# Expert rows are added to a DRAM table by an accumulating indirect DMA instead of by a matmul

## The chip, the cores and the metric

One core of one Trainium2 chip runs the whole program in one launch. The metric is device time in microseconds (us), lower is better: the median of three runs. A profiled execution gives the trace that is read here; it has a time of its own, which stands beside its span below.

## The reference

Two layers. Each mixes 256 tokens of width 1024 by four groups of attention, adds a projection and normalises, and then runs a mixture of experts. Only that last part is touched by the change:

```
scores = sigmoid(x @ w_router); sel = top 8 of (scores + router_bias) of 64 experts
gates  = scores[sel] / sum(scores[sel]) * 2.5          # 0 for experts not chosen
routed = sum over e of ((silu(h[:, :256]) * h[:, 256:]) * gates[e]) @ w_down[e],  h = x @ w_gu[e]
x      = layer_norm(ALPHA * x + routed + shared)       # shared: one more expert, without gate
```

An expert's weights are 3 MB: w_gu is 1024 x 512 and w_down 256 x 1024, in f32.

## The kernel before

**Order of the experts.** All 64 experts are ranked by how many tokens chose them. NIT = 16 steps take four experts each, in four classes. Expert A of a step (the busiest 16) is computed densely, for all 256 tokens. Expert B (the next 16) is computed for at most 128 gathered tokens, one per partition; these are "the 128 places". Experts C1 and C2 have at most 64 tokens each and share the 128 partitions. A step therefore reads 12 pieces of 1 MB: B0, B1 (the two halves of B's w_gu), A0, C10, C20, A1, C11, C21, then the four w_down, BD, AD, C1D, C2D.

**Weights.** SyncE loads the pieces in this order into a ring of six slots (`raw`, line 540). Piece j goes into slot j % 6 and is issued when TensorE has used the piece six before it (`unit_used`). So B0 and B1 of the next step are issued once C11 and C21 of this step, which one loop of products uses (line 1044), are done with. Matmuls run in fp32r, a faster format with fewer bits; for A and B each piece is split in two: ScalarE casts it to fp32r (`high`, line 1365), VectorE subtracts that from the original (`low`, line 1717). C's products are plain f32 and read the ring directly.

**A step on TensorE** (from line 1009): B's gate and up product (line 1018), A's with A0 (lines 910 to 912), the transposes of B's activations (line 1034), C with C10 and C20 (line 1044), A with A1, C with C11 and C21, B's down product into banks 0 and 1 (line 1059), the transposes of C's activations (line 1065), A's down product into the four banks 4 to 7 that hold the sums of all tokens (line 933), `scatter(place_b, t)` (line 947), C's down product into banks 2 and 3 (line 1085), the transposes of the next B tokens `xg_b` into banks 0 and 1 (line 940), `scatter(place_c, t)`, the transposes of the next C tokens `xg_c`.

**How rows get back to their tokens.** The 128 rows of B's output stand in slot order. `place_b` is a 0/1 matrix of 128 places by 256 tokens. `scatter` multiplies it with the output and adds to the banks of sums: 2 tiles x 2 halves x 2 parts = 8 matmuls of 512 columns. The two parts are `o_hi`, the ScalarE cast of the output (lines 1404 and 1406 for B, 1413 and 1415 for C), and `o_lo`, the rest, by VectorE (`out_lo`, line 1745). B and C use the same `o_hi` and `o_lo`, one after the other.

**The order on the other engines** is written out by hand, and each engine runs it in order. VectorE near the end of a step: `low(it, AD)`, C's activation `a_c` (line 1776), `out_lo` for B, `low(it+1, B0)`, `low(it+1, B1)`, `out_lo` for C, the low part of the gathered B tokens (line 1725), `low(it+1, A0)`, then the next step with `places` (lines 1736, 1737). ScalarE: the two casts of B's output, the copy `at_c`, `high(it+1, B0)`, `high(it+1, B1)`, the two casts of C's output, the cast of the gathered tokens (line 1371). GpSimd, in the experts' part, only gathers the next step's tokens from the DRAM table `x_rows` (lines 657, 659), after `tokens` on VectorE has made the indices (lines 1692 to 1696). Its DMAs run on queue q0 (software), SyncE's on q1, and both on the same 16 DMA engines.

Of the kernel before, what the change touches and what calls it, by code (L numbers as in the profile page):

```python
# [19 lines left out]
F32 = mybir.dt.float32  # L20
F32R = mybir.dt.float32r
I32 = mybir.dt.int32
U32 = mybir.dt.uint32
# [4 lines left out]
P = 128  # L28
# [8 lines left out]
def build(nc, x, w_in, b_forget, mla_q_norm, mla_kv_norm, w_mla_uq, w_mla_ukv, t5_rel_bias,  # L37
# [71 lines left out]
    with ctx:  # L109
# [92 lines left out]
        token_b = sb("token_b", [P, 1], U32, where=mo)  # L202
        token_c = sb("token_c", [P, 1], U32, where=mo)
        ranked = sb("ranked", [NE, 2, SEQ], where=mo)
        by_expert = sb("by_expert", [NE, 2, SEQ], where=mo)
# [4 lines left out]
        rank = sb("rank", [NE, 1], where=mo)  # L210
        perm = sb("perm", [NE, NE], where=mo)
        sh_down = sb("sh_down", [P, UNIT_F], where=list(mo))
        sh_down_r = sb("sh_down_r", [P, UNIT_F], F32R, where=mo)
        assert mo[0] <= nc.sbuf_usable_end, (mo[0], nc.sbuf_usable_end)
        assert shared_end <= nc.sbuf_usable_end, (shared_end, nc.sbuf_usable_end)
# [58 lines left out]
        ps = ctx.enter_context(nc.psum_tensor("ps", [P, 8, 512], F32))  # L274
        x_rows = nc.dram_tensor("x_by_token", (SEQ, D), F32, kind="Internal").ap()
        t5_dram = nc.dram_tensor("t5_by_distance", (NH, HANKEL), F32, kind="Internal").ap()
# [122 lines left out]
        b_half_ps = layer_sem("b_half_ps", NIT)  # L399
        b_out_hi_sb = layer_sem("b_out_hi_sb", 2 * NIT)  # L400
        b_out_sb = layer_sem("b_out_sb", 2 * NIT)
# [3 lines left out]
        b_added = layer_sem("b_added", NIT)  # L405
        tile0_done = layer_sem("tile0_done", 1)
# [193 lines left out]
        def _(pool):  # L600
# [5 lines left out]
            pool.memset(ones[:], 1.0).then_inc(consts_built, 1)  # L606
            pool.iota(token_row[:], [[1, SEQ]], base=0, channel_multiplier=0, allow_small_or_imprecise_dtypes=True)
            pool.iota(slot_col[:, 0:1], [[0, 1]], base=1, channel_multiplier=1, allow_small_or_imprecise_dtypes=True)
# [8 lines left out]
            for c, (base, step) in enumerate(((0, 1), (NIT, 1), (2 * NIT, 2), (2 * NIT + 1, 2))):  # L617
# [10 lines left out]
            pool.affine_select(out=head_rows[:], in_=head_rows[:], compare_op=ALU.not_equal, fill=1.0, base=0,  # L628
                               pattern=[[-1, NH], [0, P]], channel_multiplier=1).then_inc(consts_built, 1)
            with pool.Fori(0, DEPTH) as layer:  # L630
                def split_lo(k, before):

                    for half in range(2):
                        full, hi, lo = half_of(k, half)
                        pool.wait_ge(w_hi_ready, done(layer, w_hi_ready, before + half + 1))
                        pool.tensor_tensor(lo, full, hi, ALU.subtract).then_inc(w_lo_ready, 1)  # L636
# [16 lines left out]
                pool.sem_inc(pool_turn, 1)  # L653
                with pool.Fori(0, NIT) as it:
                    pool.wait_ge(token_ready, done(layer, token_ready, it + 1))
                    pool.sem_inc(pool_turn, 1)
                    pool.indirect_dma_start(xg_b[:], None, x_rows, bass.IndirectOffsetOnAxis(ap=token_b[:, 0:1], axis=0))\  # L657
                        .then_inc(xg_b_loaded, 16)
                    pool.indirect_dma_start(xg_c[:], None, x_rows, bass.IndirectOffsetOnAxis(ap=token_c[:, 0:1], axis=0))\
                        .then_inc(xg_c_loaded, 16)  # L660

        @prog.tensor
        def _(pe):
# [45 lines left out]
            with pe.Fori(0, DEPTH) as layer:  # L709
# [299 lines left out]
                def step(it, final):  # L1009
# [102 lines left out]
        def _(act):  # L1112
# [6 lines left out]
            with act.Fori(0, DEPTH) as layer:  # L1119
# [268 lines left out]
                def step(it, final):  # L1388
# [14 lines left out]
                    act.wait_ge(b_half_ps, done(layer, b_half_ps, it + 1))  # L1403
                    nc.scalar.copy(o_hi[:, 0:512], ps[:, 0, :]).then_inc(b_out_hi_sb, 1)
                    act.wait_ge(unit_used, used(layer, it, BD))
                    nc.scalar.copy(o_hi[:, 512:D], ps[:, 1, :]).then_inc(b_out_hi_sb, 1)
                    act.wait_ge(c_t_ps, done(layer, c_t_ps, it + 1))
# [22 lines left out]
        def _(dve):  # L1430
            nc.vector.memset(zeros[:].bitcast(F32), 0.0)
            dve.wait_ge(consts_built, 6)

            def layer_norm(layer, t, bank, signal, roots):

                xt = x_tok[:, t, :]
                nc.vector.scalar_tensor_tensor(xt, xt, ALPHA, ps[:, bank:bank + 2, :].rearrange("p a n -> p (a n)"),
                                               ALU.mult, ALU.add)
# [16 lines left out]
            with dve.Fori(0, DEPTH) as layer:  # L1455
# [181 lines left out]
                for t in range(NT):  # L1637
                    dve.wait_ge(outproj_ps, done(layer, outproj_ps, 1 + NOUT * t))
                    layer_norm(layer, t, OUT_BANK[t], x_mid, 2 + t)
                for b in range(4):  # L1640
# [48 lines left out]
                def tokens():  # L1689

                    for i, row in enumerate((row_b, row_c)):
                        nc.vector.scalar_tensor_tensor(found[:, i, :], row[:, 1, :], slot_col[:, i:i + 1], token_row[:],
                                                       ALU.is_equal, ALU.mult, accum_out=token[:, i:i + 1])
                    dve.drain()
                    nc.vector.tensor_copy(token_b[:], token[:, 0:1])
                    nc.vector.tensor_copy(token_c[:], token[:, 1:2]).then_inc(token_ready, 1)  # L1696

# [50 lines left out]
                def step(it, final):  # L1748

                    places(place_b, row_b, gate_b, 0).then_inc(place_b_ready, 1)  # L1750
                    dve.wait_ge(xc_ps, done(layer, xc_ps, it + 1))
                    places(place_c, row_c, gate_c, 1).then_inc(place_c_ready, 1)
# [9 lines left out]
                    if not final:  # L1762
# [28 lines left out]
                for t in range(NT):  # L1791
                    if t == 0:
                        dve.wait_ge(tile0_done, done(layer, tile0_done, 1))
                    else:
                        dve.wait_ge(moe_done, done(layer, moe_done, 1))
                    layer_norm(layer, t, 4 + 2 * t, x_next, 4 + t)

# [51 lines left out]
```

## Time and profile before

| | us |
|---|---|
| median of 3 runs (1814.83 to 1820.38) | 1816.24 |
| the profiled execution | 1813.22 |
| its span | 1811.4 |
| TensorE busy (share of the span) | 1712.4 (95%) |
| VectorE busy | 986.2 (54%) |
| ScalarE busy | 768.0 (42%) |
| GpSimd busy | 227.4 (13%) |
| DMA, mean rate over the span | 281 GB/s |
| software queue q0, share of the 16 DMA engines | 6.0% |

The busy time of an engine is a union of its instructions; a busy TensorE is not one at its peak. The two stretches with the experts run from about 210 to 905 us and from about 1120 to 1800 us. Idle time of an engine matters only where something that sets the end waits for it.

### The profile page before, as it was taken

Reading aid. Unit: us, or ns where it says so; the run is one execution under the profiler, and the core shown is the slowest. Engines: PE = TensorE matmul, PEld = TensorE weight load, DVE = VectorE, ACT = ScalarE, POOL = GpSimd, SP = SyncE. Lnnn points to the kernel's source line nnn. Section 1 sums busy time; section 2 is a strip of 40 time slices with the busy share of each in tenths; the row PEclk is TensorE's granted clock in tenths of the full one; section 3 lists DMA queues with packets and bytes.
Section 4 is the critical chain, followed back from the end, with each engine's and each line's share of the span. In section 5 each row is a group of like instructions: output and inputs, shape, how many; then the busy total and the mean of one; then the engine's idle time right before and its main releaser. Section 6 shows DMA issues by size and latency. Waiting matters only on the chain.

```text
span 1811.4 us, 29520 instructions
## 1 busy us (share of the span) xinstructions
PE 1712.4 (95%) x10302; PEld 1302.3 (72%) x10302; DVE 986.2 (54%) x1441; ACT 768.0 (42%) x1020; POOL 227.4 (13%) x160
## 2 busy tenths in 40 slices
PE   7798999999999999999979988999999999999996
PEld 6687766777777777767677876777776777777774
DVE  2746455555555555555457555555555555555554
ACT  4464333443444434444346634443444444334331
POOL 6380000000000000000144700000000000000000
PEclk8898999999999999999989989999999999999998
DMA  8232699889899989888853228888888898888983
GB/s 286 85 130 65 222 337 328 331 332 333 334 338 332 335 333 335 333 330 320 290 173 114 97 70 325 330 334 336 336 332 335 317 327 336 330 322 334 330 322 116
DMA packets 136091, 509.26 MB, mean 281 GB/s; under 512 B 11588, under 2 KB 50920, under 8 KB 102760
## 3 DMA queue, kind: packets, MB, share of 16 engines
q1 hardware_dynamic: 122288, 467.77, 70.0%
q0 software_dynamic: 9792, 35.66, 6.0%
q10 hardware_dynamic: 3960, 5.17, 0.9%
q8 instruction: 30, 0.49, 0.1%
q14 instruction: 21, 0.17, 0.0%
HBM read 505.14 MB, written 3.41 MB: 281 GB/s over the span
## 4 chain that ended last, share of the span: by engine, by line
PE 81%; DVE 7%; DMA 4%; ACT 3%; DVEq 2%; issue 2%; ACTq 0%; SPq 0%; PEldq 0%
PE ps L1044 11%; PE ps L933 10%; PE ps L1018 10%; PE ps L910 7%; PE ps L947 7%; PE ps L911 7%; PE ps L912 7%; PE ps L1085 6%; PE ps L694 5%; PE ps L1059 5%; DMA raw<-in_w_exp_down_dram 2%; PE ps L940 2%; PE ps L826 1%; DVE o_lo L1745 1%; DMA raw<-in_w_exp_gu_dram 1%
## 5 line engine op out<-in xcount | busy, mean ns | idle before, releaser
L1717 DVE TENSOR_TENSOR raw_r<-raw,w_hi 128x2048 fp32r<-128x2048 f32 x192 | 439.9, 2292 | 397.6 <-ACT w_hi L1365 397.6
L1365 ACT CAST w_hi<-raw 128x2048 fp32r<-128x2048 f32 x192 | 365.7, 1906 | 286.7 <-DMA raw<-in_w_exp_down_dram 175.5
L910 PE MATMUL ps<-x_hi,w_hi 128*128 128x256 f32 x1088 | 311.4, 286 | 1.8 <-DVE x_lo L1643 1.8
L911 PE MATMUL ps<-x_lo,w_hi 128*128 128x256 f32 x1088 | 306.9, 282 | 0.0
L912 PE MATMUL ps<-x_hi,raw_r 128*128 128x256 f32 x1088 | 306.2, 281 | 0.0
L1044 PE MATMUL ps<-raw,xc 128*64 128x512 f32 x1024 | 233.8, 598 | 0.0
L910 PEld LDWEIGHTS ps<-x_hi,w_hi 128*128 128x128 f32 x1088 | 206.6, 190 | 31.4 <-issue 30.1
L911 PEld LDWEIGHTS ps<-x_lo,w_hi 128*128 128x128 f32 x1088 | 207.9, 191 | 1.5
L912 PEld LDWEIGHTS ps<-x_hi,raw_r 128*128 128x128 f32 x1088 | 206.7, 190 | 0.0
L657 POOL DMA_INDIRECT xg_b<-x_by_token,token_b x32 | 30.1, 940 | 1248.2 <-DVE token_c L1696 1248.2
L1044 PEld LDWEIGHTS ps<-raw,xc 128*64 128x64 f32 x1024 | 67.8, 136 | 119.4 <-issue 115.0
L1745 DVE TENSOR_TENSOR o_lo<-ps,o_hi 128x512 fp32r<-128x512 f32 x128 | 87.8, 688 | 58.2 <-ACT o_hi L1415 24.3
L933 PE MATMUL ps<-w_hi,a_hi 128*128 128x512 f32 x272 | 112.2, 413 | 6.3 <-DVE a_lo L1703 6.3
L1085 PE MATMUL ps<-raw,at_c 128*64 128x512 f32 x512 | 116.9, 598 | 0.0
L933 PE MATMUL ps<-w_hi,a_lo 128*128 128x512 f32 x272 | 107.9, 397 | 0.0
L1018 PE MATMUL ps<-w_hi,xb_hi 128*128 128x512 f32 x256 | 102.5, 401 | 1.3 <-DVE xb_lo L1725 1.3
L933 PE MATMUL ps<-raw_r,a_hi 128*128 128x512 f32 x256 | 101.0, 395 | 0.0
L1018 PE MATMUL ps<-raw_r,xb_hi 128*128 128x512 f32 x256 | 100.5, 392 | 0.0
L1018 PE MATMUL ps<-w_hi,xb_lo 128*128 128x512 f32 x256 | 99.8, 390 | 0.0
L1085 PEld LDWEIGHTS ps<-raw,at_c 128*64 128x64 f32 x512 | 33.9, 136 | 66.6 <-issue 66.6
L636 POOL TENSOR_TENSOR raw_r<-raw,w_hi_odd 128x1024 fp32r<-128x1024 f32 (+1 forms) x28 | 68.6, 2471 | 63.5 <-ACT w_hi_odd L1126 63.5
L694 PE MATMUL ps<-x_hi,raw_r 128*128 128x256 f32 (+2 forms) x256 | 74.9, 293 | 0.0
(314 smaller groups left out, 2962.3 us busy)
## 6 DMA issues: line engine op xcount, KB each, us to landing
raw<-in_w_exp_gu_dram SPq DMA_DIRECT2D x256, 1024.0 KB, 6.4
raw<-in_w_exp_down_dram SPq DMA_DIRECT2D x128, 1024.0 KB, 7.5
raw<-in_w_in_dram SPq DMA_DIRECT2D x22, 1024.0 KB, 5.8
raw<-in_w_out_dram SPq DMA_DIRECT2D x8, 1024.0 KB, 5.1
row_b<-gates_by_rank SPq DMA_DIRECT2D x30, 256.0 KB, 5.7
row_c<-gates_by_rank SPq DMA_DIRECT2D x60, 128.0 KB, 5.3
raw<-in_w_sh_gu_dram SPq DMA_DIRECT2D x4, 1024.0 KB, 5.4
row_a<-gates_by_rank SPq DMA_DIRECT2D x32, 128.0 KB, 8.1
```

The costliest lines, as they stand in the source:

```text
L694: last = nc.tensor.matmul(o, a, b, start=(c == 0 and i == 0), stop=(c == KC - 1 and i == 2))
L910: nc.tensor.matmul(o, h, x_hi[:, c, :], start=(first and i == 0), stop=False, skip_group_check=True)
L911: nc.tensor.matmul(o, h, x_lo[:, c, :], start=False, stop=False, skip_group_check=True)
L912: last = nc.tensor.matmul(o, l, x_hi[:, c, :], start=False, stop=(final and i == 3), skip_group_check=True)
L933: last = nc.tensor.matmul(ps[:, 4 + 2 * t + half, :], lhs, rhs, start=False, stop=False, skip_group_check=True)
L947: last = nc.tensor.matmul(ps[:, 4 + 2 * t + half, :], place[:, t * P:(t + 1) * P], part[:, half * 512:(half + 1) * 512], start=False, stop ...
L1018: last = nc.tensor.matmul(ps[:, 2, :], a[:, c, :], b[:, i, :], start=(c == 0 and k == 0), stop=(c == KC - 1 and k == 2))
L1044: last = nc.tensor.matmul(ps[HALF * h:HALF * (h + 1), 3, :], xc[:, c, HALF * h:HALF * (h + 1)], piece_slot(j % RING, u)[:, i, :], start=(c ...
L1085: last = nc.tensor.matmul(ps[HALF * h:HALF * (h + 1), 2 + half, :], at_c[:, c, HALF * h:HALF * (h + 1)], piece_slot(j % RING, 2)[:, c, hal ...
L1365: nc.scalar.copy(w_hi[CAST[j] % 3][:], raw[:, j % RING, 0:UNIT_F]).then_inc(hi_done, 1)
L1717: nc.vector.tensor_tensor(raw_r[:, s, 0:UNIT_F], raw[:, s, 0:UNIT_F], w_hi[CAST[j] % 3][:], ALU.subtract)\
L1745: nc.vector.tensor_tensor(o_lo[:, part], ps[:, bank + half, :], o_hi[:, part], ALU.subtract)\
```

## The change

B's output no longer goes through `place_b` in 15 of the 16 steps of a layer. ScalarE copies it as f32 into a tile of its own, `o_b`. VectorE computes for each place a row number `token_out`: the token's, or for an empty place a spare row of its own behind the table. GpSimd adds the 128 rows of `o_b` to a DRAM table `added_rows` with one indirect DMA with `compute_op=add`. The table is cleared from `zeros` at the start of each layer; some spare rows are set once. After the 15th scatter GpSimd loads the table (1 MB) into `added`, and in the last step VectorE forms ALPHA * x + added before the layer norm, which then has scale 1. The last step keeps the product. For the spare rows, token numbers are counted from -256 and 256 is added where a row number is wanted; an empty place gathers a zero row behind `x_rows`.

```diff
+            pool.sem_inc(o_b_free, START[o_b_free])
+            pool.wait_ge(zeros_ready, 1)
+            pool.dma_start(x_rows[SEQ].rearrange("(p n) -> p n", n=P), zeros[0:D // P, :].bitcast(F32)).then_inc(spare_row_stored, 16)
+            pool.dma_start(added_rows[SEQ + 1:SEQ + 1 + P, :].rearrange("p (c n) -> p c n", n=P),
+                           zeros[:].bitcast(F32).unsqueeze(1).to_broadcast([P, KC, P])).then_inc(spare_row_stored, 16)
+            pool.wait_ge(spare_row_stored, 32)
             with pool.Fori(0, DEPTH) as layer:
+                for t in range(NT):
+                    pool.dma_start(added_rows[t * P:(t + 1) * P, :].rearrange("p (c n) -> p c n", n=P),
+                                   zeros[:].bitcast(F32).unsqueeze(1).to_broadcast([P, KC, P])).then_inc(sums_cleared, 16)
...
+                gather(0)
+                with pool.Fori(0, NIT - 1) as it:
+                    gather(it + 1)
+                    pool.wait_ge(o_b_ready, done(layer, o_b_ready, it + 1))
+                    pool.sem_inc(pool_turn, 1)
+                    pool.indirect_dma_start(added_rows, bass.IndirectOffsetOnAxis(ap=token_out[:, 0:1], axis=0), o_b[:], None,
+                                            compute_op=ALU.add).then_inc(o_b_added, 16)
+                    pool.wait_ge(o_b_added, done(layer, o_b_added, it * 16 + 16))
+                    pool.sem_inc(o_b_free, 1)
+                for t in range(NT):
+                    pool.dma_start(added[:, t, :], added_rows[t * P:(t + 1) * P, :]).then_inc(sums_loaded, 16)
+                pool.wait_ge(sums_loaded, done(layer, sums_loaded, 16 * NT))
...
 TensorE:
-                    pe.wait_ge(place_b_ready, done(layer, place_b_ready, it + 1))
-                    pe.wait_ge(b_out_sb, done(layer, b_out_sb, it * 2 + 2))
-                    for t in range(NT):
-                        last = scatter(place_b, t)
-                    last.then_inc(b_added, 1)
+                    if final:
+                        pe.wait_ge(place_b_ready, done(layer, place_b_ready, it + 1))
+                        pe.wait_ge(b_out_sb, done(layer, b_out_sb, 2))
+                        for t in range(NT):
+                            scatter(place_b, t)
...
                     if not final:
+                        pe.wait_ge(o_b_ready, done(layer, o_b_ready, it + 1))
                         pe.wait_ge(xg_b_loaded, done(layer, xg_b_loaded, it * 16 + 32))
 ScalarE:
+                    else:
+                        act.wait_ge(o_b_free, done(layer, o_b_free, it))
+                        nc.scalar.copy(o_b[:, 0:512], ps[:, 0, :])
+                        act.wait_ge(unit_used, used(layer, it, BD))
+                        nc.scalar.copy(o_b[:, 512:D], ps[:, 1, :]).then_inc(o_b_ready, 1)
 VectorE:
+                    if not final:
+                        dve.wait_ge(o_b_free, done(layer, o_b_free, it))
+                        nc.vector.tensor_scalar(spare[:], token[:, 0:1], 0.0, slot_col[:, 0:1], ALU.is_equal, ALU.mult)
+                        dve.drain()
+                        nc.vector.scalar_tensor_tensor(token_out[:], spare[:], float(SEQ), token[:, 0:1], ALU.add, ALU.add)
...
+                    if final:
+                        dve.wait_ge(sums_loaded, done(layer, sums_loaded, 16 * NT))
+                        for t in range(NT):
+                            nc.vector.scalar_tensor_tensor(x_tok[:, t, :], x_tok[:, t, :], ALPHA, added[:, t, :], ALU.mult, ALU.add)
...
-                    out_lo(b_out_hi_sb, b_out_sb, it, 0)
+                    if final:
+                        out_lo(b_out_hi_sb, b_out_sb, 0, 0)
```

## Rows read from the trace of the kernel before

**Rows 1.** Busy time by stretch: PE, PEld, DVE, ACT, POOL (x instructions), clock, DMA share, GB/s

```profile
210.00:860.00 650.00, 641.55 (x3611) 465.86 (x3610) 357.66 (x465) 265.85 (x285) 28.10 (x30) 1.00 0.90 332
1120.00:1755.00 635.00, 627.20 (x3522) 454.04 (x3519) 351.80 (x456) 262.81 (x282) 28.08 (x30) 1.00 0.90 333
```

**Rows 2.** The chain that ended last, 500 to 580: start, us, what

```profile
514.87 2.09 PE ps L947 x8
...
550.98 1.86 PE ps L947 x8
552.83 3.63 PE ps L1085 x16
556.49 0.59 ACT o_hi L1415
557.11 0.70 DVE o_lo L1745
557.81 0.14 issue
557.95 2.10 PE ps L947 x8
```

**Rows 3.** What line 1745 waited for, whole run: us in total, times

```profile
  ACT o_hi L1415: 24.3, 30
  ACT o_hi L1413: 18.8, 5
```

**Rows 4.** Timeline of VectorE in one step: start, us, line, what [idle before <-releaser]

```profile
553.67 2.29 DVE L1717 TENSOR_TENSOR raw_r<-raw,w_hi 128x2048 fp32r<-128x2048 f32 x1 [0.18 <-ACT w_hi L1365]
555.88 0.68 DVE L1745 TENSOR_TENSOR o_lo<-ps,o_hi 128x512 fp32r<-128x512 f32 x1
557.11 0.69 DVE L1745 TENSOR_TENSOR o_lo<-ps,o_hi 128x512 fp32r<-128x512 f32 x1 [0.54 <-ACT o_hi L1415]
...
562.66 0.35 DVE L1736 TENSOR_SCALAR place_b<-row_b,slot_col 128x256 fp32r<-128x256 f32 x1
```

**Rows 5.** Timeline of ScalarE, same step

```profile
545.20 0.58 ACT L1406 CAST o_hi<-ps 128x512 fp32r<-128x512 f32 x1 [0.77 <-PE ps L1059]
...
551.74 1.90 ACT L1365 CAST w_hi<-raw 128x2048 fp32r<-128x2048 f32 x1 [0.57 <-DMA raw<-in_w_exp_gu_dram]
554.75 0.58 ACT L1413 CAST o_hi<-ps 128x512 fp32r<-128x512 f32 x1 [1.11 <-PE ps L1085]
```

**Rows 6.** Timeline of SyncE and of TensorE, same step

```profile
542.43 3.29 SPq L540 DMA_DIRECT2D raw<-in_w_exp_gu_dram  x3
...
538.56 3.65 PE L1044 MATMUL ps<-raw,xc 128*64 128x512 f32 x16
```

**Rows 7.** DMA queue of 546 to 552: packets, MB, share of 16 engines

```profile
q1 hardware_dynamic: 339, 2.52, 100.2%
```

**Rows 8.** DMA queues and gathers of 531 to 545 (issue to landing)

```profile
q1 hardware_dynamic: 1065, 4.16, 74.6%
q0 software_dynamic: 288, 1.05, 23.3%
...
xg_b<-x_by_token,token_b POOLq DMA_INDIRECT x1, 4.8
xg_c<-x_by_token,token_c POOLq DMA_INDIRECT x1, 8.6
```

**Rows 9.** DMA queue of 172.5 to 174.5, a store of 128 rows to DRAM

```profile
q0 software_dynamic: 144, 0.52, 64.7%
```

**Rows 10.** Timeline: the index of a gather on VectorE, the gather on GpSimd

```profile
531.05 0.14 DVE L1696 CAST token_c<-token 128x1 uint32<-128x1 f32 x1
...
531.98 0.94 POOL L657 DMA_INDIRECT xg_b<-x_by_token,token_b  x1 [40.92 <-DVE token_c L1696]
```

**Rows 11.** Last step of a layer: timelines of VectorE and TensorE, then the chain

```profile
889.66 0.47 DVE L1776 SCALAR_TENSOR_TENSOR a_c<-silu_c,gate_c,ps 128x256 f32<-128x256 f32 x1
...
890.98 0.38 PE L1065 MATMUL ps<-ident,a_c 128*128 128x128 f32 x2
...
905.20 1.22 DVE x_tok L1437
```

**Rows 12.** Start: DMA queues of 10 to 38, timelines of VectorE and GpSimd

```profile
q1 hardware_dynamic: 7296, 7.37, 81.4%
q10 hardware_dynamic: 1848, 2.43, 26.3%
...
38.04 4.19 DVE L1467 TENSOR_TENSOR band_bias<-hankel,block 128x256 f32<-128x256 f32 x4 [24.65 <-DMA ln_b<-in_ln_b_dram]
...
13.23 1.04 POOL L643 CAST w_hi_even<-raw 128x1024 fp32r<-128x1024 f32 x1 [8.05 <-DMA raw<-in_w_in_dram]
```

More of the change, by code:

```diff
@@ L203, in build @@
         token_c = sb("token_c", [P, 1], U32, where=mo)
+        token_out = sb("token_out", [P, 1], U32, where=mo)
+        spare = sb("spare", [P, 1], where=mo)
         ranked = sb("ranked", [NE, 2, SEQ], where=mo)
@@ L211, in build @@
         perm = sb("perm", [NE, NE], where=mo)
+        o_b = sb("o_b", [P, D], where=list(mo))
         sh_down = sb("sh_down", [P, UNIT_F], where=list(mo))
         sh_down_r = sb("sh_down_r", [P, UNIT_F], F32R, where=mo)
+        added = sb("added", [P, NT, D], where=mo)
         assert mo[0] <= nc.sbuf_usable_end, (mo[0], nc.sbuf_usable_end)
@@ L274, in build @@
         ps = ctx.enter_context(nc.psum_tensor("ps", [P, 8, 512], F32))
[L275 removed]
+        x_rows = nc.dram_tensor("x_by_token", (SEQ + 1, D), F32, kind="Internal").ap()
+        added_rows = nc.dram_tensor("sums_by_token", (SEQ + 1 + P, D), F32, kind="Internal").ap()
         t5_dram = nc.dram_tensor("t5_by_distance", (NH, HANKEL), F32, kind="Internal").ap()
@@ L399, in build @@
         b_half_ps = layer_sem("b_half_ps", NIT)
-        b_out_hi_sb = layer_sem("b_out_hi_sb", 2 * NIT)
-        b_out_sb = layer_sem("b_out_sb", 2 * NIT)
+        b_out_hi_sb = layer_sem("b_out_hi_sb", 2)
+        b_out_sb = layer_sem("b_out_sb", 2)
         c_half_ps = layer_sem("c_half_ps", NIT)
@@ L404, in build @@
         c_out_sb = layer_sem("c_out_sb", 2 * NIT)
-        b_added = layer_sem("b_added", NIT)
+        zeros_ready = sem("zeros_ready")
+        spare_row_stored = sem("spare_row_stored")
+        sums_cleared = layer_sem("sums_cleared", 16 * NT)
+        o_b_ready = layer_sem("o_b_ready", NIT - 1)
+        o_b_added = layer_sem("o_b_added", 16 * (NIT - 1))
+        o_b_free = layer_sem("o_b_free", NIT - 1, 1)
+        sums_loaded = layer_sem("sums_loaded", 16 * NT)
         tile0_done = layer_sem("tile0_done", 1)
@@ L653, in _, with gather @@
                 pool.sem_inc(pool_turn, 1)
-                with pool.Fori(0, NIT) as it:
+                pool.wait_ge(sums_cleared, done(layer, sums_cleared, 16 * NT))
+                pool.sem_inc(pool_turn, 1)
+                def gather(it):
                     pool.wait_ge(token_ready, done(layer, token_ready, it + 1))
@@ L1403, in step @@
                     act.wait_ge(b_half_ps, done(layer, b_half_ps, it + 1))
-                    nc.scalar.copy(o_hi[:, 0:512], ps[:, 0, :]).then_inc(b_out_hi_sb, 1)
-                    act.wait_ge(unit_used, used(layer, it, BD))
-                    nc.scalar.copy(o_hi[:, 512:D], ps[:, 1, :]).then_inc(b_out_hi_sb, 1)
+                    if final:
+                        nc.scalar.copy(o_hi[:, 0:512], ps[:, 0, :]).then_inc(b_out_hi_sb, 1)
+                        act.wait_ge(unit_used, used(layer, it, BD))
+                        nc.scalar.copy(o_hi[:, 512:D], ps[:, 1, :]).then_inc(b_out_hi_sb, 1)
+                    else:
+                        act.wait_ge(o_b_free, done(layer, o_b_free, it))
+                        nc.scalar.copy(o_b[:, 0:512], ps[:, 0, :])
+                        act.wait_ge(unit_used, used(layer, it, BD))
+                        nc.scalar.copy(o_b[:, 512:D], ps[:, 1, :]).then_inc(o_b_ready, 1)
                     act.wait_ge(c_t_ps, done(layer, c_t_ps, it + 1))
@@ L1430, in _, with layer_norm @@
         def _(dve):
-            nc.vector.memset(zeros[:].bitcast(F32), 0.0)
+            nc.vector.memset(zeros[:].bitcast(F32), 0.0).then_inc(zeros_ready, 1)
             dve.wait_ge(consts_built, 6)
-            def layer_norm(layer, t, bank, signal, roots):
+            def layer_norm(layer, t, bank, signal, roots, scale):
                 xt = x_tok[:, t, :]
-                nc.vector.scalar_tensor_tensor(xt, xt, ALPHA, ps[:, bank:bank + 2, :].rearrange("p a n -> p (a n)"),
+                nc.vector.scalar_tensor_tensor(xt, xt, scale, ps[:, bank:bank + 2, :].rearrange("p a n -> p (a n)"),
                                                ALU.mult, ALU.add)
@@ L1638, in _ @@
                     dve.wait_ge(outproj_ps, done(layer, outproj_ps, 1 + NOUT * t))
-                    layer_norm(layer, t, OUT_BANK[t], x_mid, 2 + t)
+                    layer_norm(layer, t, OUT_BANK[t], x_mid, 2 + t, ALPHA)
                 for b in range(4):
@@ L1694, in tokens @@
                     dve.drain()
-                    nc.vector.tensor_copy(token_b[:], token[:, 0:1])
-                    nc.vector.tensor_copy(token_c[:], token[:, 1:2]).then_inc(token_ready, 1)
+                    nc.vector.tensor_scalar(token_b[:], token[:, 0:1], float(SEQ), None, ALU.add)
+                    nc.vector.tensor_scalar(token_c[:], token[:, 1:2], float(SEQ), None, ALU.add).then_inc(token_ready, 1)
                 def dense_gated(n):
@@ L1795, in _ @@
                         dve.wait_ge(moe_done, done(layer, moe_done, 1))
-                    layer_norm(layer, t, 4 + 2 * t, x_next, 4 + t)
+                    layer_norm(layer, t, 4 + 2 * t, x_next, 4 + t, 1.0)
 _INS = ["x", "w_in", "b_forget", "mla_q_norm", "mla_kv_norm", "w_mla_uq", "w_mla_ukv", "t5_rel_bias",
```

5 lines of the change are left out of this document (4 added, 1 removed).

## The prediction

> **What bounds the kernel now.** I read the busy time by stretch first. In the two long stretches of experts TensorE is busy 641.55 of 650 us and 627.20 of 635 us at a granted clock of 1.00, and the 16 DMA engines 0.90 of the time [rows 1]. So TensorE looks like the bound, with the DMA close behind. An average says nothing on where in a step either of them has room; for that I read the chain of waits and then the timelines of one step.
>
> The chain shows one period: the C scatter starts at 514.87 and the next one at 557.95, so a step takes 43.08 us [rows 2]. The reader is to see the hand-over at its end. TensorE finishes C's down product (line 1085), ScalarE casts the second half (0.59), VectorE takes the low part (0.70), 0.14 passes, and TensorE scatters C. The eight matmuls of the B scatter, at 550.98, take 1.86 us of the chain [rows 2]. They are what the change removes.
>
> Next I ask who would be late if C's down product came 1.86 us sooner. VectorE reaches the first half of C's `out_lo` at 555.88, straight from the split of B1 of the next step (553.67, 2.29 us), with no idle time before it [rows 4]. Only between the two halves does it wait for ScalarE, here 0.54 us. Over the whole run it waited there 24.3 us in 30 steps, 0.81 us each, and before the first half only 5 times in 32 [rows 3]. VectorE is in order, so the 0.81 us is all it can come earlier, as long as B1's split is where it is. That split is tied to a transfer: ScalarE casts B1 at 551.74, after waiting for the DMA [rows 5], and B0 and B1 are issued from 542.43, when TensorE ends the C products that begin at 538.56 and last 3.65 us [rows 6]. I call that end T0 (542.2). In times after T0: B1 cast 9.5, its split over 13.8, `o_lo` 15.2 at the earliest, C scatter 15.75. The issue at T0 does not move when the B scatter, which comes after it, goes.
>
> So the loop that would bind next is T0, transfer of B0 and B1, cast, split, `out_lo`, C scatter, and then TensorE without a gap to the next T0.
>
> **The change part by part.**
>
> *The B scatter goes* from 30 steps (15 per layer): 30 x 1.86 = 55.8 us off TensorE [rows 2]. By the loop above only 0.81 x 30 = 24.3 us of it can become time [rows 3]; for the rest TensorE would stand waiting for `o_lo`. VectorE also loses two `out_lo` of 0.69 us per step, but it waits for the DMA after them anyway, so that is worth nothing.
>
> *The scatter DMA comes*, 0.5 MB in 128 rows of 4 KB, on q0. When? ScalarE ends its second copy at 545.78 [rows 5], T0 + 3.6. From the end of `token_c` (531.19) to the gather that waits for it (531.98) pass 0.8 us [rows 10], so it is issued at T0 + 4.4, and the first of its packets I put near T0 + 6. At that moment DMA is full: from 546 to 552 q1 alone has 100.2% of the 16 engines [rows 7]. Still due are the end of B0 and all of B1, about 3 us of transfer. Whatever engine time the scatter takes before B1 has landed, B1 lands later by that, and by the loop so does everything in the step.
>
> That the two queues share the engines packet by packet, instead of q0 waiting its turn, the gathers show: in 531 to 545 q0 took 23.3% and q1 74.6%, together 98%, and the first gather landed 4.8 us after its issue with weight loads in front of it [rows 8]. The Trainium skill ("DMA: Bandwidth & Descriptors", section "Queues, rings and completion order") says that each engine takes turns between the queues it has work for, a whole packet at a time. Its example packet of 9 to 17 descriptors would let all eight rows of an engine pass in one turn; the delay of B1 would be the same.
>
> *What the scatter costs in engine time* no row shows, as the kernel has no accumulating DMA. The nearest rows: storing 128 rows to DRAM took 64.7% of 2 us = 1.29 us of all 16 engines [rows 9]; gathering 128 rows took 23.3% of 14 us, halved for two gathers = 1.63 us [rows 8]. A plain scatter would therefore cost 1.3 to 1.6. The add must read both the row in SBUF and the row in DRAM before it writes; I take two transfers, 2 x 1.29 = 2.58 us. The low end is 0, if it starts so late that B1 is already in; a high end of 4 x 1.29 = 5.2 leaves room for an adder that is slower than the copy. The same page (section "SDMA does more than copy") lists ADD as an elementwise reduce of two streams; that is the same factor of two, and no row here shows it.
>
> *Net of a step:* 2.58 - 0.81 = +1.77 us, and 30 x 1.77 = +53 us. TensorE's removed 1.86 us and the new delay of 2.58 turn into a wait of about 3.6 us before every C scatter.
>
> *New waits on `o_b_free`.* The DMA is done 4.8 to 8.6 us after issue by the gathers [rows 8], say up to 12: T0 + 9 to 16. VectorE asks for it when `place_b` is over, 562.66 + 0.8, T0 + 21 [rows 4], with all of the next B and C activations queued behind it; ScalarE and GpSimd ask later. Free, unless the add takes over 16 us. The two added one-column VectorE operations (0.15 each by the casts of [rows 10], and a drain) fall where VectorE waits 3 us for `silu_b`: nothing. `o_b_ready` before the transposes of `xg_b` is 7 us old when TensorE asks. GpSimd gathers before it scatters, so the gathers don't move.
>
> *Last step.* VectorE puts two 1024-wide operations before `a_c`. The like operation of the layer norm takes 1.22 [rows 11]. `a_c` moves from 889.66 to 892.1 and ends at 892.6, and TensorE wanted it at 890.98: 1.7 us, twice = +3.4 us. The load of the table is issued some 30 us earlier and hidden.
>
> *Start.* GpSimd now stores 0.5 MB, waits, and clears 1 MB before it can copy the first weights at 13.23 [rows 12]. From 10 to 38 the engines are full (81.4% + 26.3%), and VectorE stands from the start until 38.04 for the landing of the last parameters [rows 12]. Small packets cost 26.3% of 28 us for 2.43 MB, 3.0 us a MB; the 0.5 MB fall mostly before 10, the 1.05 MB not: 3.2 us on that landing. Bounds 0 and 10 (GpSimd issues 1024 short pieces per DMA; should that be slow, its first split is late too). In the second layer the clears fall beside the last step of the first, off the chain: 0, at most 3.
>
> *Sum:* 1813.2 + 53 + 3.4 + 3.2 = 1873 for the profiled execution. The median shown is 3.0 above that execution, so **1876 us**.
>
> **The rivals.**
>
> *A. TensorE is the bound and the DMA costs nothing on the path.* For it: 641.55 of 650 busy [rows 1]. All 1.86 us would be saved: 1816 - 55.8 + 6.6 = 1767. Against it: it needs B1's split 1 us earlier than any transfer in the trace brings it, and VectorE came to `o_lo` without a wait in 27 of 32 cases [rows 3]. Chance 0.05.
>
> *B. Faster, but by the VectorE loop only.* The scatter's packets start after B1 has landed, or fill holes. The point from which it decides is a delay of 0.81 us: below it the change is faster. At delay 0: 1816 - 24.3 + 6.6 = 1799. For it: the start near T0 + 6 is inferred, and GpSimd may need longer for an address list on the writing side; 3 us later would do. Chance 0.11.
>
> *C. Break-even.* Delay 0.6 to 0.8 us (half of a plain scatter falls in front of B1): 1810 to 1822. Chance 0.07.
>
> *D. The forecast:* delay 1.0 to 3.3 us, 1829 to 1898. Chance 0.60.
>
> *E. The adder is slow:* delay over 3.3 us, up to 5.2 and more. At 5.2, 30 x 4.4 = 132, so 1955. An even slower one runs into the `o_b_free` waits. Nothing in the trace speaks for or against. Chance 0.17.
>
> **How the numbers follow.** The most likely is D with 1876. The range of 8 in 10 leaves out A, most of B and the slow half of E: 1808 to 1945. A change within 0.3% (5.4 us) can't be told from none. Faster: A and B, 0.16. Same: C, 0.07. Slower: D and E, 0.77.
>
> **What would show it.** In the trace after: no B scatter in the loop, a period near 44.9 us instead of 43.08, ScalarE's cast of B1 near T0 + 12 instead of 9.5, and TensorE idle about 3.6 us before the first C scatter with VectorE's `o_lo` as releaser. If the cast of B1 stays at T0 + 9.5, the delay is wrong and B holds. If TensorE goes from C's down product to the C scatter with the old wait and a period of 41.2, A holds and my loop is wrong. A share of q0 in 546 to 552 gives the price of the add. `a_c` of the last step should end about 2.4 us later relative to its neighbours, and the first `band_bias` should start near 41.

## The result and the profile after

| | before | after |
|---|---|---|
| median | 1815.53 us (8 runs) | 1802.15 us (8 runs) |
| ratio | | 0.9926, 95% interval 0.9898 to 0.9953 |
| span of the profiled execution | 1811.4 | 1799.5 |

The change is 0.7% faster, some 13 us. I forecast 60 us slower, so the prediction was wrong in sign; the time that came is that of its rival B (1799). All times after T0 below are counted, as in the prediction, from the end of the products of line 1044 (1083 in the new kernel).

First the page of the kernel after, its busy times, DMA queues and two groups.

```profile
PE 1664.7 (93%) x10062; PEld 1260.4 (70%) x10062; DVE 952.0 (53%) x1445; ACT 765.8 (43%) x1020; POOL 283.5 (16%) x200
...
q0 software_dynamic: 15440, 56.11, 11.2%
...
L692 POOL DMA_INDIRECT sums_by_token<-o_b,token_out x30 | 48.2, 1607 | 379.4 <-ACT o_b L1452 379.4
...
L986 PE MATMUL ps<-o_hi,place_c 128*128 128x512 f32 x128 | 53.5, 418 | 41.4 <-DVE o_lo L1791 41.4
```

TensorE has 47.7 us less to do (1712.4 before), and the span is only 11.9 us shorter. 25 us of the rest stand in the last row: the first matmul of the C scatter now waits 41.4 us for `o_lo`, which it did for 16.2 before.

Busy time by stretch, to hold against [rows 1]: the DMA share has risen from 0.90 to 0.95 and 0.96.

```profile
210.00:860.00 650.00, 625.01 (x3519) 450.95 (x3519) 347.65 (x470) 269.71 (x290) 54.07 (x47) 0.99 0.95 347
1120.00:1745.00 625.00, 601.40 (x3401) 432.35 (x3400) 335.78 (x454) 262.07 (x282) 52.27 (x46) 1.00 0.96 351
```

The chain of one step, against [rows 2]:

```profile
502.00 8.55 DMA raw<-in_w_exp_gu_dram
510.58 1.91 ACT w_hi L1405
512.51 0.12 DVE raw_r L1763
...
514.72 1.29 DVE o_lo L1791 x2
516.01 0.14 issue
516.15 2.09 PE ps L986 x8
```

The split stands in the chain only as pieces (a wait and "issue"); the timeline of VectorE shows it whole, and both halves of `o_lo` right behind it:

```profile
512.51 2.29 DVE L1763 TENSOR_TENSOR raw_r<-raw,w_hi 128x2048 fp32r<-128x2048 f32 x1 [0.18 <-ACT w_hi L1405]
514.72 1.28 DVE L1791 TENSOR_TENSOR o_lo<-ps,o_hi 128x512 fp32r<-128x512 f32 x2
```

Before, the chain reached the C scatter from TensorE's C down product over ScalarE and one `o_lo`. Now it comes from the transfer of B1, its cast, its split and both halves of `o_lo` without a gap: the loop that the prediction named. T0 is 501.1 here; B1's cast starts at T0 + 9.4, the C scatter at T0 + 15.0. Over 28 steps the period is 42.48 us on average (43.14 before), B1 lands at T0 + 9.48 (9.35), and the C scatter starts 5.60 us after that landing (6.46).

What line 1791 (1745 before) waited for shows it too, against [rows 3]. VectorE no longer waits for ScalarE between the halves in 30 steps, but in 4.

```profile
  ACT o_hi L1459: 18.8, 3
  ACT o_hi L1461: 3.4, 4
```

Where is the scatter DMA? GpSimd issues it at 505.52, T0 + 4.4 as forecast. The DMA queues of 501 to 510, then of 510 to 516:

```profile
q1 hardware_dynamic: 688, 3.83, 102.5%
```

```profile
q1 hardware_dynamic: 316, 1.40, 59.5%
q0 software_dynamic: 144, 0.52, 43.9%
```

Up to 510 there is no packet of q0, 4.5 us after the issue. From 510 on it takes 43.9% of 6 us = 2.63 us of all engines. B1 lands at 510.56. So the add costs what was forecast (2.58), but misses B1. Read packet by packet over all 30 adds of the trace, the first packet starts 4.83 us after the issue (median; T0 + 9.3), and of 2.65 us of engine time a mean of 0.10 falls before B1 has landed.

Where the 11.9 us of the span are, from the starts of the C scatters (us): the 28 repeated steps -18.4; up to the first C scatter of the first layer +5.1 (256.43 to 261.54), although this stretch too has lost a B scatter; the last steps of the layers +3.5 and +1.5; between the layers -3.6 (243.87 to 240.26); the sum is -11.9. Of the -3.6, about 1.9 is the B scatter of the second layer's first step, which is not among the 28; the rest is no more than single traces of kernels with the same work there differ by (243.87, 241.12 and 244.79 in the kernel before and its two other orders).

### The profile page after: what moved, and what is told of

It is laid out like the page before. It is cut to its first block, busy times and chain, and to the rows that moved or that the text cites. A ratio compares the mean times of both kernels' runs of the same rounds, so it can differ in the third digit from the quotient of the medians.

```text
span 1799.5 us, 29297 instructions
## 1 busy us (share of the span) xinstructions
PE 1664.7 (93%) x10062; PEld 1260.4 (70%) x10062; DVE 952.0 (53%) x1445; ACT 765.8 (43%) x1020; POOL 283.5 (16%) x200
## 4 chain that ended last, share of the span: by engine, by line
PE 64%; DMA 15%; DVE 7%; issue 5%; ACT 5%; DVEq 2%; SPq 1%; ACTq 0%; PEldq 0%
DMA raw<-in_w_exp_gu_dram 11%; PE ps L1083 11%; PE ps L1057 10%; PE ps L949 7%; PE ps L950 7%; PE ps L951 7%; PE ps L733 6%; PE ps L986 4%; PE ps L972 4%; ACT w_hi L1405 3%; DMA raw<-in_w_exp_down_dram 3%; DVE o_lo L1791 2%; PE ps L1124 2%; PE ps L979 2%; PE ps L865 1%
## 5 line engine op out<-in xcount | busy, mean ns | idle before, releaser
L692 POOL DMA_INDIRECT sums_by_token<-o_b,token_out x30 | 48.2, 1607 | 379.4 <-ACT o_b L1452 379.4
L986 PE MATMUL ps<-o_hi,place_c 128*128 128x512 f32 x128 | 53.5, 418 | 41.4 <-DVE o_lo L1791 41.4
```

The costliest lines, as they stand in the source:

```text
L986: last = nc.tensor.matmul(ps[:, 4 + 2 * t + half, :], place[:, t * P:(t + 1) * P], part[:, half * 512:(half + 1) * 512], start=False, stop ...
```

## The experiments

Periods and landings below are means over 28 steps of the one profiled execution, times are medians of timed runs; ratios are to the kernel before on the same chip. A period also holds steps that start with TensorE's granted clock below full: one of the 28 in the change, two in run 2, seven in run 4, three in run 6. Without them the periods are 42.43 in the change, 42.19 in run 2, 42.46 in run 4 and 42.50 in run 6, each uncertain by about 0.1.

**1. The three kinds of DMA by themselves.** A small kernel, GpSimd issuing one DMA after the other, VectorE and TensorE idle.

```
pool.indirect_dma_start(table, IndirectOffsetOnAxis(index), rows_out[:], None)                      # plain store
pool.indirect_dma_start(rows_in[:], None, table, IndirectOffsetOnAxis(index))                       # gather
pool.indirect_dma_start(table, IndirectOffsetOnAxis(index), rows_out[:], None, compute_op=ALU.add)  # add
```

(The index argument is shortened; after each DMA GpSimd waits for its landing.)

> Computes nothing of the reference: it copies x out and times three DMAs of 128 rows of 4 KB on GpSimd, four of each, each waited for: a plain indirect store, a gather, and an add, first on an idle chip, then beside SyncE loading 1 MB pieces one at a time, then with three always issued. Theory G (the add's late start comes from GpSimd's own work for it): on the idle chip the add already needs about 3 us more from issue to landing than the plain store (4.5 to 5 against about 8.5), and the deeper load queue adds only the time that the engines share, about 2.5 us. Theory Q (its packets wait behind the loads that are already queued on the engines): idle, the add needs only its extra transfer, 1.3 us more than the plain store (about 6), and with three loads issued every kind, gathers too, starts 3 us or more later than with one.

Issue to landing, median of four (of two for the idle plain store, whose first two ran beside the copies of x):

| | idle | one 1 MB load issued at a time | three always issued |
|---|---|---|---|
| plain store | 3.3 us | 5.3 | 8.5 |
| gather | 3.9 | 5.5 | 8.5 |
| add | 6.0 | 5.9 | 10.2 |

Answer for the add on the idle chip, then with three loads (min/median/max), and the DMA share of the four idle adds (34.8 to 59.6):

```profile
DMA to landing us min/median/max: 5.9/6.0/6.1
...
DMA to landing us min/median/max: 9.5/10.2/10.4
```

```profile
q0 software_dynamic: 576, 2.10, 54.0%
```

Theory Q holds against G: idle, the add needs nothing near the 8.5 of theory G, and behind three loads every kind is late, the plain store by 5.2 us. The add itself costs more than Q gave it: 2.7 us over the plain store when idle, of which 0.6 is GpSimd's own instruction (1.56 against 0.95 us).

A landing is late both because the packets start late and because they share the engines. The packets themselves tell the two apart. From issue to the first packet, in us:

| | idle | one load | three loads |
|---|---|---|---|
| plain store | 1.5 | 2.6 | 4.2 |
| gather | 1.6 | 2.3 | 4.2 |
| add | 2.1 | 2.1 | 4.8 |

So the start is 1.6 to 2.6 us later with three loads than with one, less than the 3 that Q asked for; only the landings are 3.0 to 4.3 later. Counted from the end of GpSimd's instruction, the first packet comes after 0.6 to 0.7 us when idle and after 3.2 us behind three loads, for all three kinds. The add of the change (4.83 us from issue, an instruction of 1.61) has the same 3.2.

**2. Without the scatter DMA.**

```diff
-                    pool.indirect_dma_start(added_rows, ..., o_b[:], None, compute_op=ALU.add).then_inc(o_b_added, 16)
-                    pool.wait_ge(o_b_added, done(layer, o_b_added, it * 16 + 16))
```

> Leaves out the scatter DMA (B's rows are never added); all else as in the changed kernel, and o_b_free is signalled at once. Theory L (the period is set by T0, transfer of B1, cast, split, o_lo, C scatter, and the scatter's packets come too late to delay B1): the period stays within 0.2 us of the changed kernel's 42.4, the C scatter starts 5.6 us after B1's landing as there, and the time is within 6 us of 1802. Rival S (the scatter's DMA takes part of the gain in every step by sharing the engines): without it the period falls toward 41.2 and the time by 15 us or more, to below 1787.

1792.55 us, ratio 0.9872 (0.9847 to 0.9898), against 0.9926 for the change. The period is 42.29 (42.48 with the DMA), B1 lands at 9.24 (9.48), the C scatter again 5.59 after it. So the loop stands without any scatter traffic, and S's 1787 and 41.2 are not reached. But 10 us is more than L allowed, and the trace shows about 7 of them: 28 x 0.2 = 5 us go with B1's landing (0.24 earlier), and the last step of the first layer takes 44.5 instead of 46.6. The traced execution also took 1804.24 us, the longest of the five, with 250.59 us between the layers, where the change has 240.26; its span can't be compared.

**3. The scatter DMA 4 us earlier.**

```diff
-                    pool.wait_ge(o_b_ready, done(layer, o_b_ready, it + 1))
+                    pool.wait_ge(a_ready, done(layer, a_ready, it + 2))
...
-                        nc.scalar.copy(o_b[:, 0:512], ps[:, 0, :])
+                        nc.scalar.copy(o_hi[:, 0:512], ps[:, 0, :])
```

(The second half likewise; `o_b` is set to zero once, so the DMA adds zeros and B's rows are left out.)

> The same adding DMA is issued about 4 us earlier in each step, at T0, from a tile of zeros (B's rows are not added; ScalarE copies them to o_hi as before). Its packets should start near T0 + 5 in place of T0 + 9.2. Theory L: now they stand in front of B1, which lands 2.6 us later (12.0 instead of 9.4 after T0), and the period grows by the same, 42.4 to about 45.0; 30 steps give +78 us, 1802 to about 1880. Rival S (shared bandwidth as such sets the time, not the place): the same bytes at another place change nothing, 1802 within 6 us.

1920.42 us, ratio 1.0599 (1.0555 to 1.0643). B1 lands at 11.63, 2.15 later than in the change, and the C scatter comes 5.59 after it. The first packet of the add starts at T0 + 6.8 (median), and 2.46 of its 2.64 us of engine time fall before B1's landing. Place decides, not bytes: S is out. But the period grew by 4.16 us, to 46.64, not by 2.15 as L had it (1880). The timeline of TensorE in one step, then the busy time by stretch:

```profile
491.41 1.16 PE L985 MATMUL ps<-ident,xg_b 128*128 128x128 f32 x8
496.46 0.77 PE L992 MATMUL ps<-o_hi,place_c 128*128 128x512 f32 x1 [3.90 <-DVE o_lo L1797]
497.03 0.63 PE L992 MATMUL ps<-o_lo,place_c 128*128 128x512 f32 x1
```

```profile
486.00:496.00 10.00, 6.57 (x33) 3.21 (x31) 5.47 (x4) 7.01 (x7) 0.00 (x0) 0.99 1.03 365
496.00:502.00 6.00, 5.54 (x17) 4.69 (x18) 4.70 (x10) 0.58 (x2) 0.00 (x0) 0.50 0.66 279
```

After 3.9 us of idling TensorE goes on at a granted clock of 0.50, the 1.2 GHz level: a matmul of the C scatter takes 0.63 us instead of 0.39, the group of eight 3.75 instead of 2.1. In 29 of the 30 steps other than a layer's last the clock falls like this, after waits of 2.3 to 4.6 us; its mean over the 6 us from the C scatter on is then 0.50 to 0.76. The other 2.0 us of a period are there: from the C scatter to the next T0 a step takes 29.4 us on average, 27.4 in the change. With its delay right my forecast would still have been short: about 46.6 a step and not 44.9.

**4. A plain store in place of the add.**

```diff
-                    pool.indirect_dma_start(added_rows, ..., o_b[:], None, compute_op=ALU.add)
+                    pool.indirect_dma_start(added_rows, ..., o_b[:], None)
```

> The scatter DMA without the add (a plain store of the rows, so the sums are not formed). Theory G: the packets start 1.6 us after issue like those of a gather, T0 + 6, cost 8 x 0.16 = 1.3 us of the engines before B1 has landed, and the step is 1.3 us longer than now although the DMA is the cheaper one: about +35 us, 1837. Theory Q: they start as late as those of the add, T0 + 9, and the time stays within 6 us of 1802.

1811.14 us, ratio 0.998 (0.9956 to 1.0004); B1 lands at 9.53, as with the add. So it is not the add that is late: the plain store too starts behind the queued loads (8.6 us to landing, a gather 5). Its first packet comes at T0 + 8.6, not at the T0 + 6 of theory G, and 0.66 before that of the add, which is what GpSimd's instruction is shorter by (0.99 against 1.61). The time is 9 us above Q's 1802, of which at most 6 were allowed, and far from G's 1837. The period is 42.90 with a mean clock of 0.98 and 0.99 in the long stretches, 1.00 in the change; one step with its C scatter at 389.05 ran its first 5 us at 0.66. Seven of the 28 steps begin like that here, after 1.9 to 2.8 us of waiting, and one in the change. These seven take 44.2 us on average and the other 21 take 42.46, as in the change (42.43), so the whole excess over the change is the clock. Why it fell more often here is open.

**5. VectorE's order.** `out_lo` of C ahead of the split of B1, in the changed kernel and in the kernel before.

```diff
                     if not final:
                         low(it + 1, B0)
-                        low(it + 1, B1)
                     out_lo(c_out_hi_sb, c_out_sb, it, 2)
                     if not final:
                         gathered_lo(it + 1, 0)
+                        low(it + 1, B1)
                         low(it + 1, A0)
```

> The changed kernel with VectorE's order alone altered at the end of a step: low(B0), out_lo of C, the low part of the gathered tokens, and only then low(B1), low(A0). Theory L (in the changed kernel the C scatter stands 5.6 us after B1's landing because out_lo is queued behind the split of B1): the C scatter leaves B1's landing, comes about 14.0 us after T0 in place of 15.1, the period falls from 42.4 to about 41.3 and the time by about 30 us, to 1770. Rival M (the C scatter waits for the shared DMA engines or for GpSimd's scatter itself): nothing changes, 1802 within 5 us.

> The kernel before with the same new order on VectorE. Theory L (there TensorE sets the C scatter, VectorE has 0.8 us to spare): the period stays 43.1 and the time within 5 us of 1814. Rival V (the order is a gain by itself, whatever the change): the period falls by 1 us and the time by 30.

Both missed. On the change: 1806.65 us, ratio 0.994 (0.9918 to 0.9962), no gain; the number is within the 5 us of rival M, but M's mechanism is not what the trace shows. On the kernel before: 1839.27, ratio 1.0135 (1.0104 to 1.0166), slower. The C scatter did leave B1's landing (it comes 4.5 to 6.3 us after it, in the change always 5.6 to 5.8; single steps have a period of 41.3), but a second loop closed. TensorE's waits over the whole run, first in the change, then with the new order (us in total, times, longest):

```profile
PE ps L986 <- DVE o_lo L1791: 41.4, 32, 2.0
PE ps L1098 <- DVE a_lo L1749: 8.1, 9, 2.0
PE ps L1104 <- DVE a_c L1831: 5.8, 6, 1.8
```

```profile
PE ps L1098 <- DVE a_lo L1749: 25.6, 26, 2.1
PE ps L1104 <- DVE a_c L1831: 21.3, 18, 2.1
PE ps L986 <- DVE o_lo L1791: 16.3, 32, 1.5
```

The 25 us won at the C scatter (line 986) are lost again at B's down product (line 1098) and at the transposes of C's activations (line 1104). The timeline of SyncE shows why, in the kernel before (C scatter at 514.87) and in the same kernel with the new order (C scatter at 521.58):

```profile
521.59 0.33 SPq L549 DMA_DIRECT2D row_b<-gates_by_rank  x1
...
524.38 0.34 SPq L540 DMA_DIRECT2D raw<-in_w_exp_gu_dram  x1
```

```profile
529.09 0.33 SPq L549 DMA_DIRECT2D row_b<-gates_by_rank  x1
...
531.88 0.34 SPq L540 DMA_DIRECT2D raw<-in_w_exp_gu_dram  x1
```

SyncE waits for `place_c_ready` before it loads the rows, and C21 is queued behind that wait. `place_c` had moved behind the split of A0: the rows go out at +7.5 after the C scatter instead of +6.7, C21 at +10.3 instead of +9.5. From there on the engines have no room: BD's cast starts 2.50 us after the end of C10's products instead of 1.55, AD's 8.33 instead of 7.32, and TensorE waits for `a_lo` and `a_c`, both of which are queued on VectorE beside these splits.

**6. The stores of zeros moved** to where GpSimd has ended the splits of w_out.

```diff
-            pool.dma_start(x_rows[SEQ]...)              # and spare rows, before the layers, with a wait
-            pool.dma_start(added_rows[t * P:...]...)    # the clears, first thing in a layer
+            # in words: all four after the last split_lo, before x is stored; waited for behind x_rows_stored
```

> The changed kernel with the stores of zeros (the spare rows and the clears) issued by GpSimd after its last split of w_out, before the store of x, in each layer, in place of the program's start and the layer's start. Theory Z (at the start they delay the first split and the landing of the parameters; at the layer change they stand beside the last step's loads): the first row of the index scores comes back from 47.1 to about 43.5 us, the last step of the first layer from 46.6 to about 44.5, together -6 us, 1796. Rival: their cost is only the parameters' landing, 3 us, and reappears at x's store: 1800 or more.

1799.38 us, ratio 0.9905 (0.9883 to 0.9928), where the change has 0.9926: the gain of 6 is not resolved in the time. The trace has its parts: the index scores start at 43.04 (47.11 in the change, 43.49 before), the last step of the first layer takes 44.52 (46.61). But its 28 steps, which the edit leaves alone, have a mean period of 42.68, 0.2 more than in the change, and that is as much again; three of them start at a lower clock. The timeline of GpSimd in the change shows the cause at the start, beside [rows 12]:

```profile
10.51 1.73 POOL L650 DMA_DIRECT2D sums_by_token<-zeros  x2 [3.69 <-DMA sums_by_token<-zeros]
13.54 1.04 POOL L664 CAST w_hi_even<-raw 128x1024 fp32r<-128x1024 f32 x1 [1.30 <-DMA raw<-in_w_in_dram]
19.72 2.34 POOL L666 TENSOR_TENSOR raw_r<-raw,w_hi_even 128x1024 fp32r<-128x1024 f32 x1 [5.14 <-issue]
```

The cast is on time; the subtraction behind a drain comes 5.1 us after it, in the kernel before 0.15, and with the stores moved 0.15 again. The instruction of the two clears had ended 1.3 us ahead of the cast. That short distance is not the whole cause: in the second layer the same drain, the first of the layer, is long in every kernel, also in the one before, whose last gather was issued 57 us ahead:

```profile
894.11 1.04 POOL L643 CAST w_hi_even<-raw 128x1024 fp32r<-128x1024 f32 x1 [57.04 <-DMA raw<-in_w_in_dram]
898.10 2.35 POOL L645 TENSOR_TENSOR raw_r<-raw,w_hi_even 128x1024 fp32r<-128x1024 f32 x1 [2.95 <-issue]
```

There it takes 2.95 us in the kernel before, 4.50 in the change and 4.66 with the stores moved. This first drain was short (0.15) only where GpSimd had issued no DMA before it.

**7. Both of 5 and 6.**

> Both: the new order on VectorE and the moved stores of zeros. If the two are independent the time is 1802 - 32 - 6 = about 1764; if the loads of BD and AD bind next in the shorter step, half of the order's gain is lost and it is about 1780.

1801.03 us, ratio 0.9921 (0.9899 to 0.9943). Neither expectation; the second loop eats it, as in 5 (TensorE waits 26.0 us for `a_lo` in the down product of B, 8.1 in the change).

**8. A better order.** Both places ahead of A0's split, so that SyncE's wait ends earlier, not later.

```diff
 VectorE, before the steps:
-                low(0, A0)
 ... in a step, behind place_b and place_c:
+                    low(it, A0)
 ... at the end of a step:
                         low(it + 1, B0)
-                        low(it + 1, B1)
                     out_lo(c_out_hi_sb, c_out_sb, it, 2)
                     if not final:
                         gathered_lo(it + 1, 0)
-                        low(it + 1, A0)
+                        low(it + 1, B1)
```

> Leaves out the scatter DMA (B's rows are never added), and VectorE's order is low(B0), out_lo of C, the gathered tokens' low part, low(B1), both places, low(A0), so that neither out_lo waits behind B1's split nor place_c (which SyncE waits for before it may issue the rows and C21) behind A0's. Theory L2 (two loops hold the step above TensorE's own 41.2 us: B1's landing to out_lo, and place_c to SyncE's queue to BD and AD): with both opened and no scatter traffic the period falls to 41.2 to 41.5 and the time to about 1765 to 1772. Rival D (the shared engines, at 0.91 busy without the scatter, already hold it): 42 and above, 1790.

> The complete change, its stores of zeros moved, with the same order on VectorE. Theory D2 (the scatter's 2.6 us of engine time per step fills the DMA engines, 0.95 busy in the changed kernel, and BD and AD land too late): about 1.0 us per step over the run without the scatter, period near 42.2, time about 1788. If the DMA isn't what is left, the period is 41.3 and the time 1765.

> The kernel before with the same order on VectorE. With SyncE's wait for place_c no longer lengthened (the fault of the first new order, 1.0135) the time is that of before within 5 us, 1815: TensorE sets its step, so the order alone gains nothing. If it is faster by more than 5 us, the order is a gain by itself.

| | median | ratio | period | DMA share 300 to 860 |
|---|---|---|---|---|
| no scatter DMA, order of 8 | 1767.42 | 0.9729 (0.9679 to 0.9778) | 41.29 | 0.93 |
| **whole change, order of 8, zeros moved** | **1777.2** | **0.9765 (0.9721 to 0.9808)** | 41.85 | 0.96 |
| before, order of 8 | 1815.43 | 0.9979 (0.9948 to 1.001) | 43.17 | 0.90 |

L2 is confirmed: with both loops open and no scatter DMA TensorE's own 41.2 us set the step, the figure that rival A had. The order alone gains nothing on the kernel before. With the scatter DMA back the period is 0.56 us longer, half of what D2 expected; TensorE then waits 13.8 us for `a_lo` in B's down product (2.6 without it), so it is the later weights that cost. The whole computation runs in 1777 us, faster than the change (1802, intervals apart). Its chain of one step begins as before the change, at the C down product, but the `o_lo` is no longer behind a split:

```profile
502.17 3.63 PE ps L1124 x16
505.82 0.59 ACT o_hi L1461
506.44 0.70 DVE o_lo L1790
507.14 0.14 issue
507.28 2.09 PE ps L986 x8
```

## Why the prediction was wrong, point by point

- *What binds next* was right: the loop T0, B1's transfer, cast, split, `o_lo`, C scatter. The C scatter follows B1's landing by 5.59 to 5.60 us on average in the change and in runs 2, 3 and 4, at landings from 9.24 to 11.63.
- *The gain without a delay*, 0.81 us a step, was a little high: B1 landed 0.13 later, and 0.66 came (43.14 to 42.48).
- *The price of the add* was right: 2.63 us of the engines, forecast 2.58. The issue at T0 + 4.4 was right.
- **The step that failed:** "the first of its packets I put near T0 + 6". They came after 510, T0 + 9. I had taken the 1.6 us from a gather's issue to its packets as GpSimd's delay and carried it to a moment when three 1 MB loads stand in the queue and not one; the prediction gives no row for it. Run 1 shows that as its cause: from issue to the first packet the add needs 2.1 us idle and 4.8 behind three loads, and 4.83 in the change. From this one step followed the delay of B1 (+2.58 forecast, +0.13 measured) and with it the sign: 30 x (2.58 - 0.81) forecast, 28 x -0.66 measured. That early packets would have cost more than forecast, run 3 shows.
- Rival B had the time, and its condition, packets that start 3 us later, came true (T0 + 9.3). Its reason did so only in part: of the 3.3 us over my T0 + 6, GpSimd's longer instruction is 0.7 (1.61 against the gather's 0.94), the wait behind the loads the rest. That wait is 3.2 us in runs 1, 3 and 4 as well, wherever B1 stands; that it ends here just as B1 lands is luck.
- Rival C's range is off by its own sum: a delay of 0.6 to 0.8 us gives 1816 to 1822, and 1810 would be a delay of 0.4.
- The Trainium skill ("DMA: Bandwidth & Descriptors", "Queues, rings and completion order") describes engines that take turns between queues packet by packet. Once q0's packets flow both queues do get served (59.5% and 43.9% in 510 to 516); that they flow only 4.5 us after the issue with three loads ahead does not follow from it, and here the trace decides.
- *Waits on `o_b_free`*: free, as said; the scatter lands 10.1 us after issue (median of 30), VectorE asks at T0 + 19.
- *Last step*: forecast +1.7 a layer; +1.5 in the second. +3.5 in the first, where the clears of the next layer ("0, at most 3") stand beside its loads; moved away, it is 44.52 (+1.5). That they are the cause is not settled: without the scatter DMA the step takes 44.5 with the clears in place (run 2), and in the whole change of run 8, with the clears moved, 46.0.
- *Start*: forecast +3.2 through the parameters' landing, and `band_bias` did start at 40.93 (forecast 41). The first C scatter came 5.1 later although a B scatter of 1.9 before it is gone, so the start cost about 7, as GpSimd's first split was late too (TensorE waited 10.6 us for it, 5.8 before), which had been named as a bound only.
- Rival A (1767) was the wrong account of the change. Its period of 41.2 is reached once VectorE's order is altered and the scatter DMA is left out (1767); the whole computation in that order takes 1777.

## What to carry to other kernels

When work is taken off the busiest engine, ask for each instruction that the next hand-over waits for what stands ahead of it in its engine's queue: here 1.2 of the 1.86 us per step were lost to a split that nobody needed yet, and a new order on VectorE, worth nothing before the change, gave all of it back without the scatter DMA and half of it (0.63) with it. Read every wait that a reordering moves, SyncE's too, as `place_c` showed. A new DMA must be timed against the depth of the queue at its moment: the issue-to-packet time of a like DMA at a quieter moment is not a measure of it, and whether its packets come in front of or behind a load that is waited for can be worth more than its cost.

## What the runs showed of the hardware

- An indirect add of 128 rows of 4 KB to DRAM takes 2.63 us of the 16 engines in this kernel, a plain store 1.29 [rows 9]; on the idle chip the four adds took 3.35 us of them each (54.0% of 24.8 us), and issue to landing is 6.0 and 3.3 us.
- With three 1 MB loads always issued, GpSimd's DMAs land 8.5 us (plain store, gather) and 10.2 us (add) after issue, against 3.3, 3.9 and 6.0 idle. From the end of GpSimd's instruction to the first packet pass 3.2 us there, and 0.6 to 0.7 idle.
- In 29 of 30 steps of run 3 TensorE's granted clock fell to its lower level after 2.3 to 4.6 us of idling, and a step took 2.0 us more than its wait. After waits of 1.7 to 2.8 us it fell in some steps (one in the change, seven in run 4) and not in others, of up to 2.4 us.
- In run 3 GpSimd's instruction for the add took 3.33 us (median of 30) where the change has 1.61. It goes with the order in which it and a split on VectorE start. In 17 steps the split had been running for 0.08 to 0.70 us, and the instruction took 3.07 to 3.70 us; in 13 the split began at the same moment or up to 0.26 us later, and it took 1.6, although the two overlapped for 1.4 to 1.6 us there too. One step of each kind, from the timelines of VectorE and GpSimd:

```profile
479.08 2.29 DVE L1769 TENSOR_TENSOR raw_r<-raw,w_hi 128x2048 fp32r<-128x2048 f32 x1 [0.66 <-ACT w_hi L1411]
479.24 3.61 POOL L698 DMA_INDIRECT sums_by_token<-o_b,token_out  x1 [8.12 <-DVE a_lo L1755]
...
526.81 1.59 POOL L698 DMA_INDIRECT sums_by_token<-o_b,token_out  x1 [8.11 <-DVE a_lo L1755]
527.04 2.29 DVE L1769 TENSOR_TENSOR raw_r<-raw,w_hi 128x2048 fp32r<-128x2048 f32 x1 [1.04 <-ACT w_hi L1411]
```

- The first drain on GpSimd behind its DMAs lasted 5.1 us after the stores of 1024 short pieces at the start, and 2.95 us in the second layer of the kernel before, 57 us after its last gather; with no DMA before it 0.15. Why is open.
